# Sample tokens in a hybrid decoder step: states stream past tokens on four column groups, and sample attention goes by four batches

## The chip, the cores and the metric

The kernel runs on one core of a Trainium2 chip. The metric is the device time of one execution, in microseconds (us), of the whole program. All data and all products are fp32. The profile lists an fp32 matmul as two PE instructions and a transpose as one.

## The reference

A decoder step of two layers, for a prompt of 512 tokens and a sample group of 8 batches with 8 new tokens each (64 rows). Each layer mixes tokens in three ways, merges them with gates, and adds a retrieval of experts. Two of the mixers matter here. The first is a gated delta rule, with 4 heads of 128; a sample's 8 tokens are one chunk, and every batch has its own state `S` (128x128 for each head):

```python
def step(S, inp):
    intra_n, qd_n, u_n, w_n, kd_n, gl_n = inp
    v_new = u_n - jnp.einsum('bhcd,bhde->bhce', w_n, S)
    o_n = jnp.einsum('bhcd,bhde->bhce', qd_n, S) + jnp.einsum('bhcs,bhse->bhce', intra_n, v_new)
    S = S * gl_n[..., None, None] + jnp.einsum('bhcd,bhce->bhde', kd_n, v_new)
    return S, o_n
```

The second is attention in three groups (window, dilation) of 4 heads of 64; the three groups of a head slot share one softmax. A sample query sees its batch's cached rows (128, 256 and 256 of them, each batch its own) and the new rows of its batch up to itself:

```python
s = jnp.einsum('bthd,btjhd->bthj', q.astype(jnp.float32), kg) * (dh ** -0.5)
s = jnp.where(valid[None, :, None, :], s, -jnp.inf)
m = jnp.max(s, axis=-1)
p = jnp.exp(s - m[..., None])
l = jnp.sum(p, axis=-1)
o = jnp.einsum('bthj,btjhd->bthd', p, vg)
```

## The kernel before

Each layer is a row of stages. A stage is a block with a program for each engine, written out by hand; engines wait for each other by semaphores only, and between two blocks all of them meet. The order of the work on an engine is the order of the code. The stages are: the input projection and the chunk matrices of the delta rule; the **recurrence block** of the delta rule (lines 868 to 1153); the projection for attention (`window_in`); prompt attention (`window_prompt`, lines 1349 to 1482); **sample attention** (`window_samples`, lines 1488 to 1662); pooling; output projection and experts.

**Recurrence block.** PE walks through four prompt tiles: `carried(n)` (L888) multiplies the turned `w` by the state, DVE makes the new values from it (L1076), `states(n)` (L901) and `outputs(n)` (L911, L912) use them, DVE forms the next state (L1087), ACT takes squares (L1039), `turns(n)` (L923) turns the scaled rows and DVE gates them (L1108). The sample work stands between these steps. `sample_carried` (L932) is, for each of 4 heads and 8 batches, one product with the batch's 128x128 state `st` as the weights and 8 token columns moving. ACT copies its 128x256 result to `ws`. `sample_values` (L939, L940) sums two products for each head, the second one turning `ws`; ACT copies to `sample_new`. `sample_outputs` (L948, L950) has again 32 products with a state as weights and 8 columns moving, and one more for each head. `sample_states(u)`, u = 0 to 7 (half a head each, L965), makes the state's update by four products with `kdm` as weights, which POOL spreads from the keys for one head at a time (L1011). POOL multiplies the states by their decay (L1016, `decayed`), after `sample_outputs`, since that is the last reader of the old states. DVE adds the update (L1116), and SP stores it.

**Gates.** The gates' projection (3072 columns of `w_in`) is spread over both attention stages as filler for PE: 48 halves of 8 products each (`project`, L1196), 32 of them in `window_prompt` and 16 in `window_samples`. Every half goes to PSUM bank 7, ACT copies it (L1207), POOL stores each pair (L1183) and loads a next unit of weights (L1178).

**Sample attention.** For each batch SP loads the cached keys (`kc`, L1518, ring of four), PE turns ten 128x128 tiles (`keys`, L1533) into three banks, ACT copies them (`kTc`, L1605), and PE makes ten products with a key tile as weights and 16 columns moving, the batch's queries of two heads held apart (`cached_scores`, L1543). DVE gathers them in `sT` (L1639). Then, for each head h, `rows(h)` turns the scores to 64 rows of tokens (L1554) and adds the products with the new keys (L1556); DVE adds the mask and takes the maximum (L1647 to L1651), ACT the exponentials (L1613), DVE normalises (L1659), PE turns back (L1576, L1578), ACT copies (L1624, L1625), and PE multiplies by the values: three products (L1589) and for each batch and tile one with 64 columns of `vc` as weights and 8 columns moving (L1593, 40 for each head). One gate half stands in front of each of these steps. All loads of cached keys and values start in this stage.

## Time and profile before

| | us |
|---|---|
| median of the runs | 5566.54 (5565.68 to 5567.77) |
| profiled execution, its own time | 5569.33 |
| span of the profiled execution | 5567.5 |
| recurrence block, layer 0, from PE's first product to the next block's first load | 314.82 to 389.87 |
| sample attention, layer 0, between the last product of prompt attention and the first of pooling | 762.63 to 907.47 |
| recurrence block, layer 1, PE's first to last product | 3079.48 to 3149.31 |
| sample attention, layer 1 | 3527.15 to 3672.35 |

A profile row of the time line reads: start in us from the span's start, us that it lasted, engine, line of the code, operation, what is written and read, size, count of instructions merged in the row, and in brackets how long the engine had been idle and what released it. PE is the matmul engine; its granted clock is 1.0 for 2.4 GHz and 0.5 for 1.2 GHz. "PEq" and "POOLq" are the engines' own sequencers, and as the releaser of a stage's first row they stand for the meeting of the engines between two blocks.

### The profile page before, as it was taken

Reading aid. Unit: us, or ns where it says so; the run is one execution under the profiler, and the core shown is the slowest. Engines: PE = TensorE matmul, PEld = TensorE weight load, DVE = VectorE, ACT = ScalarE, POOL = GpSimd, SP = SyncE. Lnnn points to the kernel's source line nnn. Section 1 sums busy time; section 2 is a strip of 40 time slices with the busy share of each in tenths; the row PEclk is TensorE's granted clock in tenths of the full one; section 3 lists DMA queues with packets and bytes.
Section 4 is the critical chain, followed back from the end, with each engine's and each line's share of the span. In section 5 each row is a group of like instructions: output and inputs, shape, how many; then the busy total and the mean of one; then the engine's idle time right before and its main releaser. Section 6 shows DMA issues by size and latency. Waiting matters only on the chain. (4 is left out here: it accounts for less than half of the span.)

```text
span 5567.5 us, 50907 instructions
## 1 busy us (share of the span) xinstructions
PE 4800.1 (86%) x17538; PEld 2847.5 (51%) x17538; DVE 2992.0 (54%) x7268; ACT 1248.5 (22%) x3127; POOL 1558.2 (28%) x1422
## 2 busy tenths in 40 slices
PE   7889999999998787777788899999999988777776
PEld 5775777765444332332167757777654443223321
DVE  4522213225776789975455222132266677999654
ACT  2211221102222233321112112111022222333211
POOL 0321100003444444443304121000034444444442
PEclk9989998999999999999999899999999999999999
DMA  2212241317999999999812222423199999999997
GB/s 99 76 55 77 65 145 64 127 46 299 414 409 409 421 421 421 421 418 422 346 61 77 67 68 69 144 73 127 31 355 412 408 413 421 421 421 420 416 421 307
DMA packets 338620, 1432.14 MB, mean 257 GB/s; under 512 B 27388, under 2 KB 156278, under 8 KB 190442
## 3 DMA queue, kind: packets, MB, share of 16 engines
q0 software_dynamic: 177376, 1268.07, 55.8%
q1 hardware_dynamic: 155054, 157.63, 8.8%
q10 hardware_dynamic: 5932, 3.19, 0.2%
q8 instruction: 139, 2.28, 0.2%
q14 instruction: 119, 0.97, 0.0%
HBM read 1400.16 MB, written 49.44 MB: 260 GB/s over the span
## 5 line engine op out<-in xcount | busy, mean ns | idle before, releaser
L2427 PE MATMUL ps<-early,diag 128*128 128x512 f32 (+1 forms) x3584 | 1703.6, 624 | 380.7 <-ACT diag L2341 380.2
L2244 POOL DMA_INDIRECT early<-in_peer,ids x896 | 989.7, 1105 | 1808.2 <-PE ps L2427 1225.9
L2427 PEld LDWEIGHTS ps<-early,diag 128*128 128x128 f32 (+1 forms) x3584 | 665.3, 193 | 1375.8 <-issue 735.3
L2269 DVE SCALAR_TENSOR_TENSOR early<-early,rows 128x1024 f32<-128x1024 f32 x896 | 1083.6, 1223 | 438.7 <-DMA early<-in_peer,ids 437.2
L2427 PE MATMUL ps<-late,diag 128*128 128x512 f32 (+1 forms) x1024 | 493.8, 629 | 144.5 <-ACT diag L2341 144.3
L2341 ACT ACTIVATE diag<-consts_sb,weight 128x128 f32<-128x128 f32 (+1 forms) x1152 | 392.8, 388 | 705.3 <-DVE weight L2279 703.6
L2427 PEld LDWEIGHTS ps<-late,diag 128*128 128x128 f32 (+1 forms) x1024 | 184.1, 188 | 451.6 <-ACT diag L2341 238.7
L1196 PE MATMUL ps<-hT,gate_ring 128*128 128x288 f32 x1536 | 414.5, 425 | 0.0
L2333 ACT ACTIVATE gel<-dot 128x2 f32<-128x2 f32 x576 | 117.2, 203 | 1276.6 <-DVE early L2269 964.3
L2244 POOL DMA_INDIRECT late<-in_peer,ids x256 | 282.8, 1105 | 348.6 <-PE ps L2427 312.9
L2269 DVE SCALAR_TENSOR_TENSOR late<-late,rows 128x1024 f32<-128x1024 f32 x256 | 309.4, 1223 | 121.1 <-DMA late<-in_peer,ids 120.8
L1196 PEld LDWEIGHTS ps<-hT,gate_ring 128*128 128x128 f32 x1536 | 295.9, 198 | 97.6 <-issue 18.7
L1291 PE MATMUL ps<-ring,hT 128*128 128x384 f32 x768 | 257.3, 496 | 27.5 <-DMA ring<-in_w_in 24.3
L2363 PE MATMUL ps<-late 128*128 128x288 f32 x1024 | 259.3, 408 | 5.4 <-ACT late L2014 5.4
L2363 PEld LDWEIGHTS ps<-late 128*128 128x128 f32 x1024 | 195.1, 191 | 78.3 <-issue 23.3
L1458 DVE TENSOR_TENSOR sc<-ps,consts_sb 128x256 f32<-128x256 f32 (+3 forms) x96 | 43.9, 458 | 347.9 <-PE ps L1410 249.3
L1183 POOL DMA_DIRECT2D gate_rows<-gate_out x48 | 27.3, 568 | 719.7 <-ACT gate_out L1207 719.7
L1291 PEld LDWEIGHTS ps<-ring,hT 128*128 128x128 f32 x768 | 147.2, 194 | 131.2 <-DMA ring<-in_w_in 24.9
L359 PE MATMUL ps<-hT,ring 128*128 128x288 f32 x512 | 169.2, 412 | 4.2 <-PEq L275 3.6
L2279 DVE TENSOR_TENSOR weight<-gel,gates 128x2 f32<-128x2 f32 x576 | 94.1, 163 | 145.9 <-ACT gel L2333 140.0
L360 PE MATMUL ps<-hT,ring 128*128 128x288 f32 x512 | 167.5, 409 | 0.0
L1790 PE MATMUL ps<-hT,slot 128*128 128x288 f32 x384 | 126.9, 413 | 2.7 <-PEq L275 2.7
(362 smaller groups left out, 5644.0 us busy)
## 6 DMA issues: line engine op xcount, KB each, us to landing
gate_ring<-in_w_in POOLq DMA_DIRECT2D x48, 512.0 KB, 4.6
ring<-in_w_in SPq DMA_DIRECT2D x12, 1536.0 KB, 6.6
slot<-in_w_branch SPq DMA_DIRECT2D x16, 1152.0 KB, 6.1
ring<-in_w_in SPq DMA_DIRECT2D x8, 2048.0 KB, 9.2
late<-in_peer_query SPq DMA_DIRECT2D x32, 512.0 KB, 11.5
early<-in_peer,ids POOLq DMA_INDIRECT x896, 19.2
gate_rows<-gate_out POOLq DMA_DIRECT2D x48, 288.0 KB, 2.4
slot<-gate_rows SPq DMA_DIRECT2D x16, 864.0 KB, 8.0
```

Of the source, the lines that this page charges most:

```text
L359: nc.tensor.matmul(part_a(g, u), weights(k), rhs(k)[:, 0:HALF], start=k == 0, stop=k == nk - 1)
L360: last = nc.tensor.matmul(part_b(g, u), weights(k), rhs(k)[:, HALF:TOK], start=k == 0, stop=k == nk - 1)
L1196: last = nc.tensor.matmul(g.ps[:, 7, 0:HALF], self.ring[:, i % GATE_RING, k, :], g.hT[:, k, at:at + HALF], start=k == 0, stop=k == KT - 1)
L1291: last = nc.tensor.matmul(g.ps[0:P, u % 4, 0:WB], g.hT[:, k, cols(n)], w[:, k, :], start=k == 0, stop=k == KT - 1)
L1790: nc.tensor.matmul(bank_a(p), weights, g.hT[:, k, 0:HALF], start=k == 0, stop=k == KT - 1)
L2244: pool.indirect_dma_start(place(q), None, table_rows, bass.IndirectOffsetOnAxis(ap=ids[:, n, c:c + 1], axis=0)).then_inc(s.pair[PLACE[q]], 16)
L2269: nc.vector.scalar_tensor_tensor(out=up, in0=up, scalar=1.0, in1=rows[:, n, :], op0=ALU.mult, op1=ALU.mult, accum_out=dot[:, i % 2, k:k + ...
L2279: nc.vector.tensor_tensor(weight[:, i % 2], gel[:, i % 2], gates[:, n, c0:c0 + GROUP], ALU.mult).then_inc(s.weighted, 1)
L2333: nc.scalar.activation(gel[:, i % 2], dot[:, i % 2], ACT.Gelu).then_inc(s.gelus, 1)
L2341: nc.scalar.activation(diag[:, q % DIAGS, 0:ROWS[n]], table(g, "ident" if ROWS[n] == P else "ident2"), ACT.Copy, scale=weight[:, i % 2, k: ...
L2363: last = nc.tensor.matmul(g.ps[:, 4 + i % 2, 0:HALF], late.ring[:, u % Q_RING, k, :], late.hT[:, k, a * HALF:(a + 1) * HALF], start=k == 0 ...
L2427: ins = nc.tensor.matmul(g.ps[0:r, 2 * (n % 2) + m, :], diag[:, q % DIAGS, 0:r], place(q)[:, D + m * 512:D + (m + 1) * 512], start=False, ...
```

## The change

1. **Recurrence block.** In `sample_carried` and in a new step `sample_queries` the operands change places: 32 token columns are the weights (8 of them are the batch's own, the other 24 belong to neighbours and are not used), and the 128x128 state moves. The four batches of a half go to the four groups of 32 PSUM partitions, one after the other. A new table `select` picks the wanted rows: two products of 512 columns in `sample_values`, and two of 64 columns for each head in `sample_outputs`. ACT copies four 128x512 blocks where it copied one 128x256. The last reader of the old states is now `sample_queries`.
2. **State updates.** `spread` builds, for half of the batches at a time, the new values of all heads apart from each other (32 partitions, 2048 elements each), and `sample_states(u)` is one product of 512 columns for each half head. POOL decays heads 0 and 1 ahead of the two spreads, and 2 and 3 after them.
3. **Sample attention by four batches.** A unit u is four batches and two heads: 128 rows (batch c on partitions 32c to 32c+31, of which 16 are used). In `scores` the 32 columns of queries are the weights and the turned keys (128 columns) move; the scores come out as rows, so that `sT`, `rows` and L1639 go. `first`, `exps`, `normalise` work on 128x736 instead of 64x832, four times. `turn` has five 128x128 transposes and three products, `values` three products and 20 with 128 columns of weights and 32 moving.
4. **Keys** are turned by four tiles at a time into two banks, in turns copied by ACT and by DVE.
5. **Loads.** Keys of batches 0 to 2 and the values of the first half are loaded by SP in `window_prompt`; the others in sample attention, through a ring of three.
6. **Gates.** 16 halves as before, but five of them come last in the block, and the odd ones from the ninth on go to bank 0.

The diff, cut to its core:

```diff
-    ws = low[:, 2048:2048 + H * NS].rearrange("p (h c) -> p h c", h=H)
+    carried_rows, query_rows = vrow[:, 0:2], vrow[:, 2:4]
+    select = table(g, "select").rearrange("p (a c) -> p a c", a=2)
+    window = lambda half, c: slice((half * 4 + c) * NT - 24 * half, (half * 4 + c) * NT - 24 * half + 32)
+    sample_bank = (5, 7)
...
-    kdm = lowm[0:NS, 0:2048].rearrange("p (i b d) -> p i b d", i=2, b=NB)
+    spread_new = lowm[0:NS, 0:2048].rearrange("p (h b e) -> p h b e", h=H, b=4)
...
+            def sample_rows(of):
+                for half in range(2):
+                    for h in range(H):
+                        for c in range(4):
+                            last = nc.tensor.matmul(g.ps[32 * c:32 * c + 32, sample_bank[half], h * P:(h + 1) * P], of(h)[:, window(half, c)],
+                                                    st[:, h, 4 * half + c], start=True, stop=True)
+                last.then_inc(s.pe_b, 1)
+
             def sample_carried():
                 pe.wait_ge(s.loaded, 64)
                 pe.wait_ge(s.act_a, 5)
+                pe.wait_ge(s.u_copied, 4)
+                sample_rows(lambda h: wT[:, 2048 + h * NS:2048 + (h + 1) * NS])
+
+            def sample_queries():
+                pe.wait_ge(s.act_b, 2)
+                sample_rows(lambda h: cc[:, h, SEQ:TOK])
...
+            def sample_values():
+                for half in range(2):
+                    nc.tensor.matmul(g.ps[0:NS, 6, :], select[:, half], carried_rows[:, half], start=half == 0, stop=False)
                 for h in range(H):
-                    for b in range(NB):
-                        c = h * NS + b * NT
-                        last = nc.tensor.matmul(g.ps[:, 5, c:c + NT], st[:, h, b], wT[:, 2048 + c:2048 + c + NT], start=True, stop=True)
+                    last = nc.tensor.matmul(g.ps[0:NS, 6, h * P:(h + 1) * P], heads_of(invT, 4)[:, h], row(vrow, 4)[:, h], start=False,
+                                            stop=h == H - 1)
                 last.then_inc(s.pe_b, 1)
 
-            def sample_values():
-                pe.wait_ge(s.act_b, 1)
-                pe.wait_ge(s.u_copied, 3)
-                for h in range(H):
-                    nc.tensor.matmul(g.ps[0:NS, 6, h * P:(h + 1) * P], heads_of(invT, 4)[:, h], row(vrow, 4)[:, h], start=True, stop=False)
-                    last = nc.tensor.matmul(g.ps[0:NS, 6, h * P:(h + 1) * P], ws[:, h], ident(g), start=False, stop=True)
-                last.then_inc(s.pe_b, 1)
...
             def sample_outputs():
-                pe.wait_ge(s.act_b, 2)
-                pe.wait_ge(s.u_copied, 4)
+                pe.wait_ge(s.act_b, 5)
                 for h in range(H):
                     c = h * NS
                     nc.tensor.matmul(g.ps[:, 7, c:c + NS], sample_new[:, h], heads_of(dec, 4)[:, h], start=True, stop=False)
-                    for b in range(NB):
-                        last = nc.tensor.matmul(g.ps[:, 7, c + b * NT:c + (b + 1) * NT], st[:, h, b], cc[:, h, SEQ + b * NT:SEQ + (b + 1) * NT],
-                                                start=False, stop=b == NB - 1)
+                    for half in range(2):
+                        last = nc.tensor.matmul(g.ps[:, 7, c:c + NS], query_rows[:, half, h * P:(h + 1) * P], select[:, half],
+                                                start=False, stop=half == 1)
...
             def sample_states(u):
                 h, half = u // 2, u % 2
-                pe.wait_ge(s.pool_a, h + 1)
+                own = slice(32 * half, 32 * half + 32)
+                pe.wait_ge(s.pool_a, half + 1)
                 if u >= 2:
                     pe.wait_ge(s.dve_c, u - 1)
-                for b in range(4):
-                    last = nc.tensor.matmul(g.ps[:, 5 + half, b * P:(b + 1) * P], kdm[:, h % 2, 4 * half + b], sample_new[:, h],
-                                            start=True, stop=True)
-                last.then_inc(s.pe_a, 1)
+                nc.tensor.matmul(g.ps[:, 5 + half, :], krow[own, 4, h * HD:(h + 1) * HD], spread_new[own, h].rearrange("p b e -> p (b e)"),
+                                 start=True, stop=True).then_inc(s.pe_a, 1)
...
             carried(2)
+            sample_queries()
             sample_values()
...
-                nc.gpsimd.tensor_tensor(kdm[:, h % 2], bc(row(krow, 4)[:, h], 1, NB), bc(table(g, "own", NS), 2, HD), ALU.mult
+            def spread(half):
+                own = slice(32 * half, 32 * half + 32)
+                belongs = table(g, "own", NS)[own, 4 * half:4 * half + 4]
+                new = sample_new[own].unsqueeze(2).broadcast_to([32, H, 4, HD])
+                nc.gpsimd.tensor_tensor(spread_new[own], new, belongs.unsqueeze(1).unsqueeze(3).broadcast_to([32, H, 4, HD]), ALU.mult
                                         ).then_inc(s.pool_a, 1)
 
             def decayed(h):
                 k = 16 + h * NB
                 nc.gpsimd.tensor_tensor(st[:, h], st[:, h], bc(lastg[:, k:k + NB], 2, HD), ALU.mult).then_inc(s.st_scaled, 1)
 
+            pool.wait_ge(s.pe_b, 2)
+            decayed(0)
+            decayed(1)
+            pool.wait_ge(s.act_b, 5)
+            pool.wait_ge(s.st_scaled, 2)
             spread(0)
+            pool.wait_ge(s.pool_a, 1)
             spread(1)
-            pool.wait_ge(s.pe_b, 3)
-            for h in range(H):
-                decayed(h)
-                if h + 2 < H:
-                    pool.wait_ge(s.pe_a, 2 * h + 2)
-                    spread(h + 2)
+            pool.wait_ge(s.pool_a, 2)
+            decayed(2)
+            decayed(3)
...
             act.wait_ge(s.pe_b, 1)
-            nc.scalar.copy(ws, bank(5, P, NS)).then_inc(s.act_b, 1)
+            for half in range(2):
+                nc.scalar.copy(carried_rows[:, half], g.ps[:, sample_bank[half], :]).then_inc(s.act_b, 1)
...
-            pe.wait_ge(s.gate_copied, self.l * 2 * GATE_UNITS + v)
+            pe.wait_ge(s.gate_copied, self.l * 2 * GATE_UNITS + v - behind)
...
+    places = g.space(AT_CACHES)
+    caches = Caches(g, t, l, places)
+    window_prompt(nc, g, l, vals, qkT, gates, caches, g.space(AT_PROMPT))
     clear_semaphores(nc, g)
...
+        @block.sync
+        def _(sp):
+            caches.ahead(sp)
...
+    def load_values(self, sp, half, sem):
+        for j, (i, m) in enumerate(CACHE_TILES):
+            sp.dma_start(self.values[half][:, :, j], cache_rows(self.t, self.l, i)[half * QUAD:(half + 1) * QUAD, m * P:(m + 1) * P, 1]
+                         .rearrange("b p c -> p b c")).then_inc(sem, 16)
+
+    def ahead(self, sp):
+        for b in range(KEY_RING):
+            self.load_keys(sp, b, self.g.s.loaded2)
+        self.load_values(sp, 0, self.g.s.loaded2)
+        sp.wait_ge(self.g.s.loaded2, 48 * KEY_RING + 80)
...
+            for b in range(KEY_RING, NB):
+                sp.wait_ge(s.pe_a, (10 * (b - KEY_RING) + 9) // 4 + 1)
+                caches.load_keys(sp, b, key_rows[b % KEY_RING])
+                if b == KEY_RING + 1:
+                    caches.load_values(sp, 1, s.loaded2)
...
+            def keys(q):
+                if q >= 2:
+                    pe.wait_ge((s.act_a, s.dve_a)[q % 2], (q - 2) // 2 + 1)
+                for e in range(4 * q, 4 * q + 4):
+                    b, (j, pair) = e // 10, divmod(e % 10, 2)
+                    if b >= KEY_RING and (e % 10 == 0 or e == 4 * q):
+                        pe.wait_ge(key_rows[b % KEY_RING], 48 * (b // KEY_RING))
+                    last = nc.tensor.transpose(g.ps[:, q % 2, (e % 4) * P:(e % 4 + 1) * P],
+                                               caches.keys[:, b % KEY_RING, j, pair * P:(pair + 1) * P], ident(g))
+                last.then_inc(s.pe_a, 1)
...
+                for j, (i, m) in enumerate(CACHE_TILES):
+                    for c in range(QUAD):
+                        to = g.ps[32 * c:32 * c + 32, bank + j // 4, (j % 4) * P:(j % 4 + 1) * P]
+                        nc.tensor.matmul(to, apart[:, 2 * i + pair, half * QUAD + c].rearrange("p a t -> p (a t)"),
+                                         kTc[:, 10 * c + 2 * j + pair, :], start=True, stop=True)
+                for i in range(3):
+                    for c in range(QUAD):
+                        to = g.ps[32 * c:32 * c + 32, bank + 1, P + i * S_OWN:P + (i + 1) * S_OWN]
+                        last = nc.tensor.matmul(to, apart[:, 2 * i + pair, half * QUAD + c].rearrange("p a t -> p (a t)"),
+                                                qkT_s[:, 6 + 2 * i + pair, half * S_OWN:(half + 1) * S_OWN], start=True, stop=True)
                 last.then_inc(s.pe_b, 1)
...
+            def turn(u):
+                half = S_UNITS[u][0]
+                bank, own = score_bank(u), slice(half * S_OWN, (half + 1) * S_OWN)
+                pe.wait_ge(s.dve_d, u + 1)
                 for j in range(5):
+                    nc.tensor.transpose(g.ps[:, bank + j // 4, (j % 4) * P:(j % 4 + 1) * P], sc[:, u % 2, j * P:(j + 1) * P], ident(g))
                 for i in range(3):
+                    last = nc.tensor.matmul(g.ps[own, bank + 1, (1 + i) * P:(2 + i) * P],
+                                            sc[:, u % 2, S_CACHED + i * S_OWN:S_CACHED + (i + 1) * S_OWN], ident(g), start=True, stop=True)
+                last.then_inc(s.pe_d, 1)
...
+                    nc.tensor.matmul(g.ps[:, 2, 0:P], vals_s[own, i * 256 + pair * P:i * 256 + (pair + 1) * P], pT[own, u % 2, 5 + i, :],
+                                     start=i == 0, stop=False)
+                for c in range(QUAD):
                     for j in range(5):
+                        last = nc.tensor.matmul(g.ps[:, 2, 32 * c:32 * c + 32], caches.values[half][:, c, j, pair * P:(pair + 1) * P],
+                                                pT[:, u % 2, j, 32 * c:32 * c + 32], start=False, stop=j == 4 and c == QUAD - 1)
...
```

In the recurrence block, PE's order is as follows around the sample steps (`mid` holds the turned `w`, `st` the states, `cc` the queries, `vrow` the copied rows, `low` the prompt's state). Before:

```order
L901 MATMUL ps<-low_1083,krow_1080 128x128 x4
L932 MATMUL ps<-mid_1087,st_1089 128x8 x32
L911 MATMUL ps<-low_1083,cc_95 128x128
L912 MATMUL ps<-low_1083,dec_1082 128x128
...
L923 MATMUL ps<-consts_sb,kbg_1088 128x128 x4
L888 MATMUL ps<-low_1083,mid_1087 128x128 x4
L939 MATMUL ps<-vrow_1081,invT_1086 64x128
L940 MATMUL ps<-consts_sb,low_1083 64x128
...
L948 MATMUL ps<-dec_1082,kbg_1088 128x64
L950 MATMUL ps<-cc_95,st_1089 128x8 x8
```

Now:

```order
L907 MATMUL ps<-low_1083,krow_1080 128x128 x4
L936 MATMUL ps<-st_1089,mid_1087 32x128 x32
L917 MATMUL ps<-low_1083,cc_95 128x128
L918 MATMUL ps<-low_1083,dec_1082 128x128
...
L929 MATMUL ps<-consts_sb,kbg_1088 128x128 x4
L894 MATMUL ps<-low_1083,mid_1087 128x128 x4
L936 MATMUL ps<-st_1089,cc_95 32x128 x32
L952 MATMUL ps<-vrow_1081,consts_sb 64x512 x2
L954 MATMUL ps<-vrow_1081,invT_1086 64x128 x4
...
L962 MATMUL ps<-dec_1082,kbg_1088 128x64
L964 MATMUL ps<-consts_sb,vrow_1081 128x64 x2
```

The products with the queries moved forward, in front of `sample_values`, and what is left in `sample_outputs` is three products for each head where there were nine.

In sample attention, PE's first part (`kc` holds cached keys, `kTc` turned ones, `apart` the queries, `sT` the gathered scores). Before:

```order
L1533 MATMUL ps<-consts_sb,kc_4660 128x128 x20
L1196 MATMUL ps<-hT_91,gate_ring_2799 128x288 x8
L1543 MATMUL ps<-apart_4663,kTc_4662 128x16 x10
L1533 MATMUL ps<-consts_sb,kc_4660 128x128 x10
...
L1554 MATMUL ps<-consts_sb,sT_4664 64x128 x5
L1556 MATMUL ps<-qkT_s_2798 64x64 x3
```

Now:

```order
L1596 MATMUL ps<-consts_sb,kc_3436 128x128 x28
L1220 MATMUL ps<-hT_91,gate_ring_2784 128x288 x8
L1596 MATMUL ps<-consts_sb,kc_3436 128x128 x12
...
L1617 MATMUL ps<-kTc_4669,apart_4668 32x128 x20
L1622 MATMUL ps<-qkT_s_2783,apart_4668 32x32 x12
```

A gate half stood between the turning of a batch's keys and its scores, for each batch; now seven groups of keys come in a row, and two units of scores follow one another after ten groups.

The end of sample attention on PE (`pT` holds the turned probabilities, `vc` the cached values). Before:

```order
L1196 MATMUL ps<-hT_91,gate_ring_2799 128x288 x8
L1576 MATMUL ps<-consts_sb,sc_4665 128x64 x5
L1578 MATMUL ps<-consts_sb,sc_4665 64x64 x3
...
L1589 MATMUL ps<-pT_4666,vals_s_2797 64x64 x3
L1593 MATMUL ps<-pT_4666,vc_4661 64x8 x40
L1504 UNCONDITIONAL_BRANCH
```

Now:

```order
L1631 MATMUL ps<-consts_sb,sc_4666 128x128 x5
L1633 MATMUL ps<-consts_sb,sc_4666 32x128 x3
L1220 MATMUL ps<-hT_91,gate_ring_2784 128x288 x8
L1647 MATMUL ps<-pT_4670,vals_s_2782 128x128 x3
L1651 MATMUL ps<-pT_4670,vc_3438 128x32 x20
L1220 MATMUL ps<-hT_91,gate_ring_2784 128x288 x40
L1570 UNCONDITIONAL_BRANCH
```

The block ended with the products with the values; now five gate halves (40 products) stand behind them.

## Rows read from the trace of the kernel before

**Rows 1.** Stretches: us, busy time of PE, PEld, DVE, ACT, POOL, clock, DMA, GB/s.

```profile
315.00:391.00 76.00, 65.71 (x418) 61.37 (x417) 24.37 (x48) 12.51 (x46) 14.94 (x8) 0.76 0.21 60
763.00:908.00 145.00, 133.81 (x917) 112.58 (x918) 16.95 (x39) 24.11 (x56) 9.15 (x15) 0.87 0.39 126
3079.00:3156.00 77.00, 65.76 (x418) 61.46 (x418) 24.34 (x48) 12.51 (x46) 15.22 (x8) 0.76 0.22 59
3527.00:3673.00 146.00, 134.06 (x920) 112.66 (x919) 17.25 (x40) 24.11 (x56) 9.14 (x16) 0.87 0.39 126
```

**Rows 2.** Time line of PE in the recurrence block of layer 0.

```profile
328.05 11.13 PE L932 MATMUL ps<-mid,st 128*128 128x8 f32 x64
...
344.92 0.43 PE L939 MATMUL ps<-vrow,invT 64*64 64x128 f32 x2
...
348.80 0.39 PE L911 MATMUL ps<-low,cc 128*128 128x128 f32 x2
...
351.53 0.63 PE L923 MATMUL ps<-consts_sb,kbg 128*128 128x128 f32 x4 [0.78 <-DVE oa L1108]
...
353.34 1.95 PE L950 MATMUL ps<-cc,st 128*128 128x8 f32 x16
...
361.72 3.58 PE L950 MATMUL ps<-cc,st 128*128 128x8 f32 x16
365.15 2.05 PE L901 MATMUL ps<-low,krow 128*128 128x128 f32 x8
...
369.77 0.63 PE L923 MATMUL ps<-consts_sb,kbg 128*128 128x128 f32 x4 [0.17 <-DVE oa L1108]
```

**Rows 3.** Time line of all engines, the end of the same block.

```profile
365.38 1.90 POOL L1016 TENSOR_TENSOR st<-st,lastg 128x1024 f32<-128x1024 f32 x1 [46.83 <-PE ps L950]
...
372.46 1.89 POOL L1011 TENSOR_TENSOR lowm<-krow,consts_sb 64x1024 f32<-64x1024 f32 x1 [5.18 <-PE ps L965]
...
384.79 0.69 DVE L1116 TENSOR_TENSOR st<-st,ps 128x512 f32<-128x512 f32 x1 [1.02 <-PE ps L965]
389.87 1.01 SPq L389 DMA_DIRECT2D ring<-in_w_in  x2
```

**Rows 4.** Time line of PE in the projection: products that go to PSUM halves by turns.

```profile
420.67 2.82 PE L1295 MATMUL ps<-ring,hT 128*64 128x192 f32 x32
423.80 2.50 PE L1291 MATMUL ps<-ring,hT 128*128 128x384 f32 x7 [0.32 <-PE ps L1295]
```

**Rows 5.** Time line of PE in sample attention of layer 0.

```profile
771.59 2.40 PE L1533 MATMUL ps<-consts_sb,kc 128*128 128x128 f32 x10 [8.96 <-DMA kc<-in_cache_win]
...
784.45 4.05 PE L1196 MATMUL ps<-hT,gate_ring 128*128 128x288 f32 x16
788.33 2.30 PE L1543 MATMUL ps<-apart,kTc 128*128 128x16 f32 x20
790.48 1.29 PE L1533 MATMUL ps<-consts_sb,kc 128*128 128x128 f32 x10
791.61 4.05 PE L1196 MATMUL ps<-hT,gate_ring 128*128 128x288 f32 x16
...
845.00 4.88 PE L1593 MATMUL ps<-pT,vc 128*64 128x8 f32 x80
...
851.85 6.42 PE L1196 MATMUL ps<-hT,gate_ring 128*128 128x288 f32 x16
```

**Rows 6.** Time line, start of sample attention, SP and ACT.

```profile
767.58 7.71 SPq L1518 DMA_DIRECT2D kc<-in_cache_win  x14
...
772.74 0.59 ACT L1605 COPY kTc<-ps 128x512 f32<-128x512 f32 x1 [12.01 <-PE ps L1533]
```

**Rows 7.** Time line, end of sample attention: the last store of gates and the next stage.

```profile
900.82 0.54 POOL L1183 DMA_DIRECT2D gate_rows<-gate_out  x1 [18.29 <-ACT gate_out L1207]
...
907.47 1.30 PE L1790 MATMUL ps<-hT,slot 128*128 128x288 f32 x2 [1.35 <-PEq L275]
```

**Rows 8.** Part 6 of the page, DMA issues: KB each, us to landing.

```profile
gate_rows<-gate_out POOLq DMA_DIRECT2D x48, 288.0 KB, 2.4
```

More of the change, by code:

```diff
@@ L117, in constants @@
     put("ident2", i[:, None] % NS == np.arange(NS)[None])
+    token = np.arange(NS)
+    first = 32 * (token % 32 // NT) + token % NT
+    put("select", np.stack([(i[:, None] == first + 24 * a) & (token // 32 == a) for a in range(2)], 1) * 1.0)
     put("own", (i[:, None] // NT == np.arange(NB)[None]) * 1.0)
@@ L1056, in _ @@
             act.wait_ge(s.pe_b, 2)
+            for half in range(2):
+                nc.scalar.copy(query_rows[:, half], g.ps[:, sample_bank[half], :]).then_inc(s.act_b, 1)
+            act.wait_ge(s.pe_b, 3)
             nc.scalar.copy(sample_new, bank(6, NS, HD)).then_inc(s.act_b, 1)
@@ L1215, in window_stage @@
     gates = Gates(nc, g, t, l, sb)
-    samples = sb.above()
+    low = sb.above()
     vals = sb("vals", [P, 4, SW])
@@ new lines, in window_samples @@
+def window_samples(nc, g, t, l, vals_s, qkT_s, gates, caches, low, high, late, slots):
+    s = g.s
+    sc, stat, apart = low("sc", [P, 2, S_WIDTH]), low("stat", [P, 2, 4]), low("apart", [P, 6, NB, QUAD, NT])
+    kTc = high("kTc", [P, 10 * QUAD, P])
+    pT = late("pT", [P, 2, 8, P])
+    key_rows = (s.slab0, s.slab1, s.map0)
+    mask = table(g, "smask")
+    first_gate = 2 * 4 * SLOTS
+    gate_bank = lambda i: 0 if i >= 9 and i % 2 else 7
+    score_bank = lambda u: 3 + 2 * (u % 2)
+    key_group = lambda q: kTc[:, 4 * (q % 10):4 * (q % 10) + 4, :]
@@ L1555, in rows @@
                 for i in range(3):
-                    last = nc.tensor.matmul(g.ps[0:NS, first + 1, P + i * NS:P + (i + 1) * NS], q_s(i, h), k_s(i, h), start=True, stop=True)
-                last.then_inc(s.pe_c, 1)
-            keys(0)
-            for b in range(NB):
-                if b + 1 < NB:
-                    keys(b + 1)
-                gates.project(pe, 2 * done + b)
-                cached_scores(b)
-            pe.wait_ge(s.dve_a, NB)
-            pe.wait_ge(s.act_a, 3 * NB)
@@ L1595, in _ @@
                 last.then_inc(s.pe_e, 1)
+            for q in range(7):
+                keys(q)
+            gate(0)
+            for q in range(7, 10):
+                keys(q)
+            gate(1)
+            scores(0)
+            scores(1)
+            gate(2)
+            for q in range(10, 13):
+                keys(q)
+            gate(3)
+            turn(0)
+            keys(13)
+            keys(14)
+            gate(4)
+            values(0)
+            keys(15)
+            keys(16)
@@ new lines, in _ @@
+            for q in (0, 2, 4, 6):
+                keys(q)
+            gate(0)
+            keys(8)
+            gate(1)
+            exps(0)
+            gate(2)
+            keys(10)
+            keys(12)
+            exps(1)
+            gate(3)
+            turned(0)
+            keys(14)
+            gate(4)
+            keys(16)
+            turned(1)
+            gate(5)
+            keys(18)
+            gate(6)
+            exps(2)
+            gate(7)
+            exps(3)
+            gate(8)
@@ L1629, in _ @@
+            turned(2)
+            gate(9)
+            turned(3)
+            for i in range(10, 2 * GATE_UNITS - first_gate):
+                gate(i)
         @block.vector
```

290 lines of the change are left out of this document (153 added, 137 removed).

## The prediction

> **What bounds the kernel now.** The page's busy shares are averages over stages with different limits, so I went to the two stages that the change touches. First the stretches [rows 1]: in the recurrence block PE is busy for 65.71 of 76 us, in sample attention for 133.81 of 145 us, and no other engine for more than 25. Layer 1 shows the same to 0.3 us, so I work out layer 0 and double it. The clock column says that PE ran at a mean of 0.76 and 0.87 there, so part of this time is work at 1.2 GHz. Then PE's time line [rows 2, 5]: the rows follow each other with hardly an idle bracket. The set-up is the same in both stages: PE is the path, and the sample steps stand in its order as plain length. Last I looked for what takes over when PE gets shorter: the state updates by DVE with POOL in front of them [rows 3], the cached keys' transfer and the keys' copies [rows 5, 6], and the last store of the gates [rows 7, 8].
>
> **Why the old products are slow.** L932 does 64 instructions with 8 columns moving and 128x128 weights. It takes 11.1 us. L950, the same form, takes 1.95 us for 16 instructions while the clock is high and 3.58 us while it is low [rows 2], which is 0.12 and 0.22 us for each. The 8 columns cost next to nothing; the change of weights does. The low clock came while PE was "busy" with such instructions: the granted clock went to 0.5 in the course of L932 and again in the course of L950. The same holds in sample attention after L1593: the gate half behind it (L1196) takes 6.42 us, against 4.05 us [rows 5].
>
> **Do column groups run side by side?** Everything hangs on this. The trace has two groups: L1295 sends 32 instructions of 192 columns by turns to two halves of PSUM, in 2.82 us, which is 0.176 us for a pair [rows 4]. A gate instruction of 288 columns takes 4.05/16 = 0.253 us [rows 5], so 192 columns one after the other would be 0.169 us each. The pair takes the time of one. Four groups are not in this trace. I take that four also share one time: 128 columns cost 128/288 x 0.253 = 0.113 us, plus 0.01 for the change of weights, 0.123 us for four instructions. The bound above is no sharing at all, 0.123 us for each. The bound below is the same 0.123 for four, since the columns must stream in any case. I take the lower end, since the row of two groups shows full sharing. The Trainium skill ("TensorE: Matmul & The Clock Gate", part 3, packing small matmuls) gives 2.38x for three column tiles of 32 with 512 columns, and no figure for four. By 0.8 of the ideal, an estimate, the sum below would be about 5 us smaller.
>
> **Recurrence block, from L932 to the last `turns`** (328.05 to 369.77, 41.7 us [rows 2]). New lengths at the full clock, in PE's order:
> - `sample_carried`: 64 instructions, 16 rounds of four: 16 x 0.123 = 2.0 us (was 11.0).
> - `outputs(1)`: 1.8, as `outputs(2)` takes at the full clock (348.80 to 350.75, where PE begins to wait, with 0.1 of pipeline). `turns(0)` 0.45, `carried(2)` 0.95.
> - `sample_queries`, new place: 2.0 us. Before it ACT must have made two copies of 128x512 (0.59 each [rows 6]), ready some 2 us earlier: hidden. If squares held ACT, PE would wait about 1 us.
> - `sample_values`: four instructions of 512 columns at 0.45 us = 1.8, and eight at 0.18 = 1.4 (an L939 pair has 0.43 us with the end of its pipeline, 0.36 without): 3.2 us (was 2.9).
> - `states(2)`, `outputs(2)`: 0.95 + 1.8. `turns(1)`: its wait for DVE stays (0.78 idle): 1.4. `carried(3)` 0.95.
> - `sample_outputs`: for each head one pair of 0.36 and four instructions of 0.12: 3.4 us (was 12.1). Its operands wait for one more ACT copy, made during `states(2)`.
> - `states(3)`, `outputs(3)`: 0.95 + 1.8 (were 4.6, at the low clock).
>
> Sum 21.7 us. PE lost 0.32 us where it went from PSUM halves back to the full width [rows 4]; four such places: 1.3 us. So 23.0 instead of 41.7: **18.7 us less**. The Trainium skill ("TensorEngine Tiling (Array Packing)", key properties) says that a change of tiling mode drains TensorE, which speaks against this change with its many switches; the 0.32 us is what the row makes of it, and by a drain twice as long the sum would be about 3 us smaller for each layer.
>
> **The rest of that block** stays as long (369.77 to 389.87). `sample_states` moves the same 512 columns for each half head as before. POOL's two spreads have 2048 elements: by L1011 (1.89 us for 1024, [rows 3]) 3.8 us each, 7.6 in all, as four of 1.89 before. POOL decays heads 0 and 1 from the end of `sample_queries` (2 x 1.90), then the spreads: the first is ready about 4 us after `sample_new`, 7 us ahead of `sample_states(0)`. DVE's order is untouched, and its chain of eight updates is what ends the block. A bound the other way: were POOL's spread on 32 partitions twice as slow, it would still be ready.
>
> **Sample attention.** PE ran from 771.59 to 906.1, 134.5 us. Now:
> - Gates: 16 halves at 4.0 = 64 us (784.45 to 788.33 is 3.9, behind values 4.05).
> - Keys: ten tiles take 1.13 us (790.48 to 791.61), so a group of four 0.45. With two banks the copies show: 0.45 + 0.2 + 0.6 (ACT, [rows 6]) or 0.7 (DVE) + 0.1 for two groups, 0.7 for each. Seven groups in a row 5.6 (with a start at the low clock and DVE's larger `apart` first), four runs of three or two 6.9: 12.5 us.
> - Scores: per unit 40 instructions of 128 columns in 10 rounds, 1.23, and 24 of 32 columns in 6 rounds at 0.08: 1.7; four units 6.8. L1543 (8 x 2.15), L1554 and L1556 go.
> - Turns: 5 x 0.113 and 6 instructions in one group at 0.12: 1.3; four 5.3.
> - Values: 40 instructions with 128 columns of weights and 32 moving. The nearest row is L1543, 2.15 us for 20 (788.33 to 790.48); with 6 more of 0.12, 5.3; four 21.2. The cost below is L1593, 0.061 each for half the weights, at which it would be 3.2.
> - Clock: the gate behind values lost 2.4 us [rows 5]. With 32 columns moving instead of 8, PE is denser; I keep 4 us of loss where there were about 11.
> - Switches: six at 0.32, 1.9.
>
> Sum 115.7, against 134.5: 18.8 us less. **Start:** the stage opens at 767.58 and PE waited for keys until 771.59 [rows 5, 6]; they are there now: 3.8 less. The load itself goes to `window_prompt`, whose DMA is mostly free; SP has nothing else there. The later loads: batch 5's keys stand on SP's queue behind five loads of values, issued about 773 to 780, needed near 789, so hidden. **End:** the last gate half now ends the stage. Its copy (0.5), POOL's issue (0.3 on) and 2.4 us to landing [rows 8] came before beneath the values (900.82, 6.65 us ahead of the next stage [rows 7]); open they put 4.5 us between PE's last and next product, where there were 1.35: 3.2 more. Net **19.4 us less**.
>
> **The sum.** 18.7 + 19.4 = 38.1 for each layer, 76 in all. The profiled execution would go from 5569.3 to 5493; on the median, which lies 2.8 us lower, to **5490**. Nothing else in the program uses these steps; the expert stages are as long as before.
>
> **The rivals.**
> - *Four groups share only in pairs.* For: two groups is all the trace shows. Rounds double: `sample_carried` and `sample_queries` +2.0 each, scores +1.6 a unit: +10.4 a layer, 5511.
> - *No sharing for 32-column groups.* The instructions then stream one by one: +5.9 twice, and scores 6.4 instead of 1.7, +18.8: +30.6 a layer, 5551. Against: L1295.
> - *The clock falls as often as before.* Values still change weights more than they stream. Then 7 to 10 us more a layer, 5507.
> - *It goes further.* Values at the lower bound (8 us a layer), no clock loss (4), or both: 5466 to 5482.
> - *Slower than before.* No sharing, and the low clock through these steps too, with the gates behind them. Then `sample_carried` and `sample_queries` are 14 us each (+24 a layer), scores 11 a unit (+38), three gates +3.4 each (+10): 72 a layer against 38 gained: 5634. It decides once the steps cost over 38 us a layer more than I took. Against: the columns that stream are then dense, and dense rows (L1196 at 784.45) have their 4.05 us.
>
> **How the numbers follow.** Forecast (5478 to 5500) 0.62; pairs 0.10; clock as before 0.10; further 0.08; no sharing 0.07; slower 0.03. The predicted time is the forecast's. The range 5466 to 5522 takes in the first four, with a little for each bound, and leaves out the two dear cases: about 0.8 once small misses at both ends are counted. A measurement of this kernel can tell about 0.2% (11 us) from no change. Faster by more than that: all but the last case and the upper end of no sharing, 0.95; within 0.02; slower 0.03.
>
> **What the profile of the changed kernel would show.** The 64 instructions of L936 in about 2 us, starts of four together; 8 us would mean no sharing. From the first `sample_carried` to the last `turns` 23 us, then about 20 us to the next block's load, ended by L1116's successor on DVE. In sample attention PE's first key product right behind the block's start, no wait for `kc`, scores of 1.7 us a unit, a gate behind values of 4 us, and about 4.5 us between the last gate half and pooling. The prediction is wrong if L936 takes over 4 us a step, if DVE's or POOL's rows end PE's waits in the middle of the recurrence, or if the gates stay at 6 us.

## The result, and the profile after

The changed kernel takes **5513.15 us** (median of 4 runs, 5511.29 to 5517.84) against 5567.16 for the kernel before on the same chip (4 runs, 5565.68 to 5577.44): ratio 0.9899, 95% interval 0.9884 to 0.9915. The profiled spans are 5567.5 and 5509.8 us, 57.7 less. The forecast was 5490, the range 5466 to 5522: the time lies inside the range, but 54 of the 76 us came.

Where the two traces differ, from PE's time lines (start of one landmark to the next, us):

| Stretch | predicted, a layer | layer 0 | layer 1 |
|---|---|---|---|
| first instruction of the recurrence to first of the next projection | -18.7 | -20.2 | -18.1 |
| that projection and prompt attention | 0 | -1.0 | -1.6 |
| prompt attention to first key product of the samples | -3.8 | -3.9 | -4.2 |
| body of sample attention | -18.8 | -12.1 | -12.2 |
| last product of the body to first of pooling | +3.2 | +4.1 | +4.2 |

These give 33.1 and 32.0. The recurrence of layer 0 began 4.1 us later than before, and the stages between and behind cost 3.7 more; so 65.1 becomes 57.3 at the last product.

The recurrence went as forecast. PE's time line of layer 0, behind [rows 2] (start us, us for the group, engine, line, tiles, shapes, count, idle time before and its releaser):

```profile
332.26 1.95 PE L936 MATMUL ps<-st,mid 128*32 128x128 f32 x64
334.14 0.49 PE L917 MATMUL ps<-low,cc 128*128 128x128 f32 x2
...
337.45 1.95 PE L936 MATMUL ps<-st,cc 128*32 128x128 f32 x64
339.34 1.93 PE L952 MATMUL ps<-vrow,consts_sb 128*64 128x512 f32 x4
341.20 1.08 PE L954 MATMUL ps<-vrow,invT 64*64 64x128 f32 x8
...
351.24 2.02 PE L907 MATMUL ps<-low,krow 128*128 128x128 f32 x8
...
355.82 0.63 PE L929 MATMUL ps<-consts_sb,kbg 128*128 128x128 f32 x4 [0.20 <-DVE oa L1132]
```

L936 is `sample_rows`: 64 instructions in 1.88 us to the next start, where L932 took 11.0 [rows 2]. One by one, the four starts of a round lie 7 ns apart and rounds follow every 0.109 us (the second after 0.133): all four groups share one time. From the first L936 to the last `turns` it is 23.6 us, where 23.0 was forecast. No idle bracket stands where PE goes to column groups and back; the 0.32 us of [rows 4] did not repeat. The clock still fell once, at the end of `sample_outputs`: L907 took 2.02 us instead of 1.16.

Not all of this gain is the new form of the products. The same stretch as a whole (us; busy time of PE, PEld, DVE, ACT, POOL; granted clock, DMA share, GB/s), first in the kernel before, then in the changed one:

```profile
328.05:369.77 41.72, 40.78 (x242) 38.46 (x241) 8.51 (x24) 5.10 (x24) 1.90 (x1) 0.71 0.01 4
```

```profile
332.26:355.82 23.56, 22.58 (x253) 19.58 (x253) 10.96 (x24) 6.83 (x26) 14.68 (x6) 0.93 0.02 7
```

At a clock of 0.71 the 41.7 us are worth 29.6 us of the full clock, and at 0.93 the 23.6 us are worth 21.9. By this estimate some 8 of the 18 us are work that is gone, and some 10 are the clock, which fell in L932 and L950 and now hardly falls here. No run measures the two apart.

In sample attention PE's first key products have no wait for `kc`, only the meeting of the engines between two blocks (`PEq`). Rows of layer 0:

```profile
750.60 2.88 PE L1596 MATMUL ps<-consts_sb,kc 128*128 128x128 f32 x12 [5.06 <-PEq L278]
...
756.21 4.05 PE L1220 MATMUL ps<-hT,gate_ring 128*128 128x288 f32 x16
760.09 1.04 PE L1596 MATMUL ps<-consts_sb,kc 128*128 128x128 f32 x8
...
761.97 4.05 PE L1220 MATMUL ps<-hT,gate_ring 128*128 128x288 f32 x16
765.95 1.30 PE L1617 MATMUL ps<-kTc,apart 128*32 128x128 f32 x40
767.06 0.37 PE L1622 MATMUL ps<-qkT_s,apart 128*32 128x32 f32 x24
...
784.64 0.93 PE L1647 MATMUL ps<-pT,vals_s 32*128 32x128 f32 x6
785.50 6.64 PE L1651 MATMUL ps<-pT,vc 128*128 128x32 f32 x40
791.96 1.95 PE L1596 MATMUL ps<-consts_sb,kc 128*128 128x128 f32 x8
793.70 1.19 PE L1631 MATMUL ps<-consts_sb,sc 128*128 128x128 f32 x5
...
800.52 4.78 PE L1651 MATMUL ps<-pT,vc 128*128 128x32 f32 x40
805.11 3.06 PE L1596 MATMUL ps<-consts_sb,kc 128*128 128x128 f32 x12
...
829.89 6.66 PE L1651 MATMUL ps<-pT,vc 128*128 128x32 f32 x40
836.36 1.31 PE L1631 MATMUL ps<-consts_sb,sc 128*128 128x128 f32 x5
...
843.96 7.04 PE L1651 MATMUL ps<-pT,vc 128*128 128x32 f32 x40
850.81 22.26 PE L1220 MATMUL ps<-hT,gate_ring 128*128 128x288 f32 x80
878.55 1.30 PE L1950 MATMUL ps<-hT,slot 128*128 128x288 f32 x2 [5.48 <-PEq L278]
```

Scores take 1.3 to 1.4 us a unit (L1617 with L1622). The same 40 values instructions (L1651) take 4.8 us once and 6.6 to 7.0 three times; eight key products behind them take 1.95 us instead of 1.09, and the first of the five gate halves at the end takes 6.57 us to the next one's start, where the three behind it take 3.88. The granted clock goes to 0.5 in the course of three of the four values steps, and at the end of the fast one, whose followers pay (3.06 us for the 12 instructions of L1596). The stretches, columns as above, first the kernel before, then the changed one:

```profile
771.00:907.00 136.00, 133.28 (x916) 112.08 (x916) 15.55 (x36) 24.11 (x56) 8.95 (x13) 0.88 0.38 125
```

```profile
750.00:874.00 124.00, 120.59 (x820) 99.34 (x820) 24.71 (x53) 18.38 (x38) 8.60 (x13) 0.88 0.32 103
```

Twelve us shorter, and the granted clock is the same 0.88 of 2.4 GHz. In the table, the row that ends at the first key product is the early loads, and the last row is the open store of the last gates, with the pause of 5.48 us in front of L1950 above.

### The profile page after: what moved, and what is told of

It reads as the page before. It is cut to its first block and busy times, and to the rows that moved or that the text cites. A ratio compares the mean times of both kernels' runs of the same rounds, so it can differ in the third digit from the quotient of the medians.

```text
span 5509.8 us, 50367 instructions
## 1 busy us (share of the span) xinstructions
PE 4729.3 (86%) x17274; PEld 2768.6 (50%) x17274; DVE 3007.9 (55%) x7296; ACT 1240.7 (23%) x3097; POOL 1542.9 (28%) x1418
## 5 line engine op out<-in xcount | busy, mean ns | idle before, releaser
L1950 PE MATMUL ps<-hT,slot 128*128 128x288 f32 x384 | 127.9, 415 | 11.0 <-PEq L278 11.0
```

The source lines that it names most:

```text
L1950: nc.tensor.matmul(bank_a(p), weights, g.hT[:, k, 0:HALF], start=k == 0, stop=k == KT - 1)
```

## Experiments

**Theory 1: the clock.** The 40 values instructions have 32 columns moving behind each 128x128 block of weights. The profile shows PE as busy there, yet the clock falls. If it falls because so few columns move, the step with more columns moving should cost no more at the full clock, and keep it. **Rival:** the step costs what it costs, about 6.6 us, and the gates behind are slow for another reason. The two differ in the gates: with the rival they stay at 22.3 us.

*e1_wide* moves all 128 columns of the four batches against every batch's weights; the products of foreign columns are never read. Same count of instructions, same weights, four times the columns.

```
-   last = nc.tensor.matmul(g.ps[:, 2, 32 * c:32 * c + 32], caches.values[half][:, c, j, ...],
-                           pT[:, u % 2, j, 32 * c:32 * c + 32], ...)
+   nc.tensor.matmul(g.ps[:, 2, P * c:P * (c + 1)], caches.values[half][:, c, j, ...],
+                    pT[:, u % 2, j, :], ...)
...
+   last = nc.tensor.matmul(spaced(slice(0, P)), vals_s[own, ...], ...)   # now behind, into blocks of 32 columns, 160 apart
```

> The changed kernel with one step made wider: in the values step of sample attention each of the 20 products moves all 128 columns of the turned probabilities instead of 32 (into four column ranges of the same bank, of which the same results are read), and the three products with the new values come last. Weights, waits, copies and order of the steps are the same; PE has four times as many columns to stream there. Theory 1 (the granted clock falls in the values steps because PE mostly changes weights there): the clock stays at 1.0 through the four values steps of each layer, each takes 5.4 to 5.8 us (they took 7.3, 5.4, 7.3 and 7.7), the steps behind them are back to their full-clock lengths, and the kernel is 16 to 24 us faster than the changed one: 5489 to 5497. Rival (the steps are long because 128 columns of weights are loaded for each product, and the low clock has another cause, such as waits): no gain, or up to 5 us slower for the columns added, 5510 to 5520.

Measured 5481.38 us (5479.26 to 5487.49), 0.9839 of the kernel before on its chip (0.9826 to 0.9852): 32 us less than the changed kernel, more than the 16 to 24 expected. Time line of PE:

```profile
780.86 4.63 PE L1649 MATMUL ps<-pT,vc 128*128 128x128 f32 x40
785.42 0.93 PE L1652 MATMUL ps<-pT,vals_s 32*128 32x128 f32 x6
786.28 1.09 PE L1597 MATMUL ps<-consts_sb,kc 128*128 128x128 f32 x8
...
837.10 19.67 PE L1220 MATMUL ps<-hT,gate_ring 128*128 128x288 f32 x80
```

and the stretch, columns as before:

```profile
746.00:857.00 111.00, 107.57 (x820) 88.66 (x820) 24.71 (x53) 18.17 (x38) 8.39 (x12) 0.98 0.35 115
```

Four times the columns cost nothing: 4.63 us for 40, against 4.78 in the one fast step of the changed kernel. The clock is 0.98 (it is low under the stage's first key products alone; from 751 us to the end of the body it is 1.00), the key products and gates behind are at 1.09 and 19.67 us. The body takes 109.9 us in both layers, 12.6 less than in the changed kernel. The rival falls. The edit also puts the three products with the new values (0.86 us) last instead of first; no run moves them alone. Of the 31 us between the profiled spans, 25.2 lie here; 3.6 are an earlier start of the recurrence (below), and 2.4 are spread over stages that the edit doesn't touch.

*e7_narrow* asks whether still fewer columns matter: only 16 columns move, and no other column is read.

```
-   ... g.ps[:, 2, 32 * c:32 * c + 32] ... pT[:, u % 2, j, 32 * c:32 * c + 32]
+   ... g.ps[:, 2, 32 * c:32 * c + 16] ... pT[:, u % 2, j, 32 * c:32 * c + 16]
```

> The changed kernel with the 20 products of the values step moving only the 16 columns of a batch that are used, instead of 32. Theory 1 (the step is bound by the change of weights, and the clock falls when few columns stream): no time saved in a step at the full clock (4.6 us for 40 instructions), and the clock is low in the values steps at least as often: 0 to 8 us more than the changed kernel. Rival (the step's length follows its columns): 5 to 10 us less.

Measured 5511.82 us (5511.02 to 5514.67), against 5511.93 (5511.53 to 5514.16) for the changed kernel beside it. Half the columns save nothing, neither at the full clock (4.58 us to the next start in the fastest step) nor at the low one, so the rival is out: from 16 to 128 columns the weights price this step. The clock fell in or at the end of all these steps, as in the changed kernel. The body takes 125.7 and 122.5 us in the two layers here, and 122.5 and 125.7 in *a1_after_again* below: how much of it is at the low clock differs from one execution to another, by about 3 us.

*a1_after_again* is the changed kernel once more, on the chip of e5, e6 and e7.

> The changed kernel as it is, for comparison on the same chip as the runs beside it: 53 to 57 us below the kernel before.

Measured 5511.93 us, which is 66 below the kernel before and not 53 to 57. The changed kernel takes what it took on the first chip (5513.15); the kernel before is slower here: 5578.2 us (5569.85 to 5584.04), against 5567.16. The ratio is 0.9885 (0.987 to 0.99). So a difference to the kernel before is known to some 10 us only.

*b1_before_wide* makes the same edit in the kernel **before**, with 64 columns moving instead of 8 in L1593, and nothing of the change.

```
-   nc.tensor.matmul(g.ps[r:r + SD, 1 + h % 2, b * NT:(b + 1) * NT], vc[:, b, j, ...], pT[:, h % 2, j, b * NT:(b + 1) * NT], ...)
+   nc.tensor.matmul(g.ps[r:r + SD, 1 + h % 2, b * NS:(b + 1) * NS], vc[:, b, j, ...], pT[:, h % 2, j, :], ...)
```

> The kernel before with one step made wider, as e1 did for the changed one: each of the 40 products of a head with the cached values moves all 64 columns of the turned probabilities instead of 8, the three products with the new values come last. Theory 1 (a PE that mostly changes weights falls to the low clock, and the steps behind pay as well): the gate halves behind the values steps go from 6.3, 5.2 and 6.7 us to 4.1, the values steps from 4.8 to 6.9 us to about 5 (64 columns take 0.056 us at 0.113 for 128, less than the 0.061 us that an instruction takes now), 10 to 13 us less a layer, 20 to 27 in all. Rival (what e1 gained is owed to the changed kernel's form of the step): no gain here, or a loss of up to 5 us for the columns added.

Measured 5546.73 us (5542.91 to 5549.07), 27 less than 5573.91, ratio 0.9951 (0.9939 to 0.9963). That is at the upper end of the 20 to 27 expected. Where [rows 5] had 4.88 and then 6.42 us:

```profile
844.15 4.88 PE L1591 MATMUL ps<-pT,vc 128*64 128x64 f32 x80
...
850.60 4.15 PE L1196 MATMUL ps<-hT,gate_ring 128*128 128x288 f32 x16
```

```profile
771.00:895.00 124.00, 121.39 (x916) 103.03 (x916) 15.54 (x36) 24.13 (x56) 8.96 (x13) 0.97 0.42 138
```

Its body takes 122.2 us, what the changed kernel's takes. So the low clock in and behind the values steps cost 12.3 us a layer before and costs 12.6 after. Without it the bodies are 122.2 and 109.9: the new form by four batches is worth 12.3 us, and in this stage the change gave back nothing of the clock.

**Theory 2: sharing.** The gain of `sample_rows` is that four groups share one time, and it rests on their order. *e4_one_group_at_a_time* sends, within each half, all of one group, then the next.

```
-                    for h in range(H):
-                        for c in range(4):
+                    for c in range(4):
+                        for h in range(H):
```

> The changed kernel with two loops exchanged in the recurrence block: the 32 products of a sample step go to the first group of 32 PSUM partitions for all four heads, then to the second, and so on, instead of to the four groups by turns. Same products, same data, same count. Theory (successive products to different column groups share their streaming time, those to the same group do not): a step of 64 instructions takes 6 to 8 us instead of 1.9, 4 to 6 us more, twice a layer; with the exchange at the three changes of group still overlapping, 16 to 24 us more in all, 5529 to 5537. Rival (the engine orders them itself, or 32-column products are short anyway): the steps stay at 1.9 us, 5513.

Measured 5519.95 us (5518.18 to 5524.79), 0.9908 (0.9893 to 0.9923).

```profile
328.92 4.33 PE L936 MATMUL ps<-st,mid 128*32 128x128 f32 x64
...
336.49 4.33 PE L936 MATMUL ps<-st,cc 128*32 128x128 f32 x64
```

2.4 us more a step, not the 4 to 6 expected, 9.5 in the four steps; the profiled spans are 8.3 apart and the medians 7 to 8 on different chips, where 16 to 24 were expected. The trace doesn't name the groups, but its starts can be read: the first four instructions follow every 0.109 us, as without sharing, and from then on they come in pairs, as if the next group began with its predecessor's fifth, so that two groups overlap. Order matters, and less than the count of groups says.

*e6_attention_only* has the recurrence of the kernel before with the changed attention.

> The kernel before with its own recurrence block and only the sample attention, the early loads and the gates of the change. By the traces the attention is worth 12 us for each layer and the recurrence 18: 24 to 27 us less than the kernel before, that is 30 to 36 more than the changed kernel. If the recurrence were worth less on its own (for instance since its gain is given back later), this one would come nearer to the changed kernel, at under 25 us from it.

Measured 5552.31 us (5549.99 to 5554.94), ratio 0.9957 (0.9944 to 0.9971): 26 less than the kernel before, as expected, and 40 more than the changed kernel, so the recurrence is worth 20 a layer, more than the 15 to 18 expected. The profiles agree: the recurrence block, up to the first product of the next projection, takes 82.1 us in both layers here, and 60.6 and 62.2 in *a1_after_again*.

**Theory 3: loads and tail.** *e5_loads_in_stage* issues the first loads of keys and values at the start of sample attention, as before the change.

```
-        @block.sync
-        def _(sp):
-            caches.ahead(sp)
...
+            for b in range(KEY_RING):
+                caches.load_keys(sp, b, key_rows[b])
+            caches.load_values(sp, 0, s.loaded2)
```

> The changed kernel with the early loads undone: the keys of batches 0 to 2 and the values of the first half are loaded by the sample attention stage itself, keys first, not by the prompt's. Theory (the stage gained the wait for keys that the trace of before shows, 8.96 us idle against 5.05 now, and nothing else is owed to the early loads): 4 us more for each layer, 8 in all, with a second place where PE may wait: batch 5's keys stand behind ten loads of values and come some 7 us later, 0 to 6 us more a layer. So 8 to 20 us more than the changed kernel. Rival (the loads land before PE's first key product anyway, since the meeting of the engines takes longer): no difference.

Measured 5531.58 us (5523.50 to 5539.95), 0.9916 (0.9903 to 0.993), 19.7 more than the changed kernel beside it, at the upper end of the 8 to 20 expected. The waits come back, on PE's time line:

```profile
754.36 2.48 PE L1595 MATMUL ps<-consts_sb,kc 128*128 128x128 f32 x10 [9.06 <-DMA kc<-in_cache_win]
...
768.99 0.87 PE L1595 MATMUL ps<-consts_sb,kc 128*128 128x128 f32 x6 [3.87 <-DMA kc<-in_cache_win]
```

The first wait ends 4.0 us later than in the changed kernel's pause of 5.06, which is the term of 3.8. The second, 3.87 us behind the first gate half, was not in that term: the new order asks for its keys sooner than they land. Of the body's 132.4 us (122.5 in the changed kernel) 4.2 are such waits, and the clock over the stretch is 0.84, not 0.88, which is most of the rest. So without the early load the change would have lost most of its gain in this stage: 19.7 us by medians, of 24 in both layers, counted from the last product of the prompt to the first of pooling.

*e2_tail* moves the last values step behind the last gate halves, so that the store of the gates is covered again.

```
-            gate(10)
-            values(3)
-            for i in range(11, 2 * GATE_UNITS - first_gate):
+            for i in range(10, 2 * GATE_UNITS - first_gate):
                 gate(i)
+            values(3)
```

> The changed kernel with the last values step of sample attention moved behind the last gate halves, where it was in the kernel before, so that the last copy, store and landing of the gates lie beneath it. Theory (the open end costs what the two traces show, 5.5 us between PE's last and next product against 1.35): 3 to 4 us less for each layer, 5505 to 5507. Rival (the pause costs nothing more than the low clock at which the values step would leave PE for the pooling stage): 0 to 2 us less in all, 5511 to 5513.

```profile
865.88 6.03 PE L1651 MATMUL ps<-pT,vc 128*128 128x32 f32 x40
...
873.49 1.30 PE L1949 MATMUL ps<-hT,slot 128*128 128x288 f32 x2 [1.59 <-PEq L278]
```

The pause goes from 5.48 to 1.59 us, 3.9 a layer. The total, 5497.37 us (5492.91 to 5500.63), 0.9863 (0.9848 to 0.9878), is some 16 less than the changed kernel's median, on another chip, and 8 below what was expected. The profiled spans are 11.2 apart, of which 7.8 is the pauses. The body of layer 1 is 3.4 shorter and the recurrence blocks together 2.7, which is no more than the same kernel varies by: in *a1_after_again* one body is 3.2 longer and the recurrence blocks together 2.8 shorter than in the first profile. So the pauses are shown, and no trace shows that the rest is owed to the edit.

*e3_both* joins e1 and e2.

> Both edits together: 128 columns moving in the values step and the last values step at the block's end. If the two causes are apart, the gains add: 5482 to 5491. If the wide products only move the fall of the clock to the steps behind, no more than one of them: 5495 or above.

Measured **5475.07 us** (5473.96 to 5477.32), 0.9825 (0.9812 to 0.9838), against 0.9839 for the wide values alone. The second edit adds 6.3 us to the first, near the 7.8 of the pauses, so the two causes are apart; the sum lies 7 us below the 5482 to 5491 expected, as the wide values alone already did. It computes all that the reference does, and beats both kernels.

## Why the prediction was right or wrong

- *Four groups share one time.* Right: 1.88 us where 2.0 was taken. The rivals with pairs or no sharing are out; e4 shows what partial sharing looks like. The Trainium skill ("TensorE: Matmul & The Clock Gate", part 3) has 2.38x for three column tiles; here four instructions took the time of one, 0.109 us, so the trace shows more sharing than that.
- *Recurrence, 18.7 less.* Right: 41.7 became 23.6 us from L932 and its successor to the last `turns`, and the whole block is 20.2 and 18.1 shorter. "The rest of that block" stayed as long to about 1 us: 18.9 us to the next block's load, against 20.1. DVE's update ends it, as forecast. The sum was made at the full clock, and the clock did stay up here; by the estimate above that is more than half of this gain.
- *Switches, 3.2 us a layer.* Too dear: 0.32 us was taken for each, and the starts show about 0.1. A gate half between full-width products takes 3.88 us to the next start (756.21 to 760.09), in front of the column groups of L1617 it takes 3.98 (761.97 to 765.95). The Trainium skill ("TensorEngine Tiling (Array Packing)", key properties) says that a mode change drains TensorE; at these switches the trace has no idle bracket, only that 0.1 us.
- *Start.* Right in size (3.9 and 4.2 for 3.8); *end*: the right mechanism, 4.1 for 3.2.
- *Scores.* 1.3 to 1.4 for 1.7 us a unit. *Values* were right at the full clock: 5.4 in e1 (780.86 to 786.28), for 5.3. The terms named beside that 5.3 (two times 2.15 and six of 0.12) make 5.0, a slip of 0.3 a step that happened to help.
- *Clock, the term that failed.* "With 32 columns moving instead of 8, PE is denser; I keep 4 us of loss where there were about 11." The loss was 12.6 us a layer, by e1, and 12.3 before, by b1: 32 columns moving did no more for the clock than 8. That is 8.6 a layer, 17 in all, the largest part of the miss in the profiled execution (57.7 for 76). The other terms of the body were together 1.8 a layer too dear. The 7.8 us outside the forecast's stages (4.1 of them in the next point) and 1 us a layer at the stage's end come on top, and about 4 us more than forecast in the recurrence, the prompt's stages and the start make up for part of them. The rival "the clock falls as often as before", given 0.10, is what happened; its 5507 lies 6 us from the measured median, which is outside the 5478 to 5500 that had 0.62. One of the prediction's own signs of being wrong came true as well: the gate half behind the last values step takes 6.57 us, where 4 was forecast.
- *Not in the sum:* the recurrence began 4.1 us later. In the profiled executions of the kernel before, b1, e1 and e4 it began 315 to 316 us from the start, in the other seven at 319 to 321, among them e6, whose recurrence is the old one. It is not an effect of the steps forecast. The traces show where it comes from: in these seven the clock, once up, falls again at 35 to 37 us, under the program's first projection, and in the four it doesn't. The same two instructions, in the kernel before and in the changed one:

```profile
35.98 0.65 PE L360 MATMUL ps<-hT,ring 128*128 128x288 f32 x2
```

```profile
38.83 1.17 PE L363 MATMUL ps<-hT,ring 128*128 128x288 f32 x2
```

Of the 4.1 us, 3.6 are there by the end of these products (45.97 against 42.38 us). Why the clock falls there in some executions stays open. *e1_wide* is one of the four, so 3.6 us of its lead in the profile is luck.

## What to carry to other kernels

When products with few moving columns stand on TensorE's path, count the weights: here these set the time, and the clock fell beneath them. Packing into column groups lets instructions share their time. Moving all the columns that lie beside the wanted ones, though they are thrown away, cost nothing here at the full clock, and kept it. Price the two apart, by the rows *behind* the step (a dense step at 4.05 or 6.4 us), before you count on either. And ask of a gain how much of it is the clock: in the recurrence that was, by estimate, more than half, in sample attention nothing.

## What the runs showed of the hardware

- Four instructions to four groups of 32 PSUM partitions started 7 ns apart and took 0.109 us together. In the order of one group at a time 64 of them took 4.33 us, 0.067 each, with two groups overlapping as the starts are read.
- 128x128 weights with 16, 32 and 128 columns moving had one price: in the step with the least low clock, 40 instructions took 4.58 us to the next start in e7, 4.49 in the changed kernel and 4.56 in e1, 0.11 us each.
- With 8 columns moving (the kernel before), 16 (e7) or 32 (the changed kernel) the granted clock went to 1.2 GHz in the course of these steps or at their end. With 64 (b1) and 128 (e1) moving it stayed at 2.4 through all four steps of both layers. The kernel before and b1 have 64 columns of weights in each product, the others 128.
- A change between full-width products and column groups of 32 took about 0.1 us, with no idle bracket.
